# A two-layer decoder step on one core: each weight unit's matmuls in two groups, each behind its own wait

## The reference

```
h = rms_norm(x, norm_g)
z = h @ w_in                       # 2048 -> 14*512 + 8 + 4*2048 columns
y_ret, y_gdn, y_sc, y_pool = four token mixers on slices of z, each times its SiLU gate
proj  = einsum('btnc,ncd->btnd', ys, w_branch)       # four branches, 512 -> 2048
gates = sigmoid(merge_logits)                        # the last 4*2048 columns of z
out   = x + sum_n(gates * proj) @ w_out              # 2048 -> 2048
```

## Time and profile before

| | |
|---|---|
| time of three runs | 2048.74, 2050.52, 2054.93 us |
| the profiled execution | span 2049.6 us from first to last instruction; its own whole time is not listed, the median of the runs is 0.9 us above this span |
| PE | busy 1992.3 us, 97% of the span, 16294 matmuls and as many weight loads |
| DVE | busy 1346.1 us, 66% |
| ACT | busy 1113.6 us, 54% |
| transfers | 348 MB, 170 GB/s in the mean |
| granted TensorE clock | 0.993 of full in the mean |

### The profile page before, as it was taken

One profiled execution on the slowest core, in us unless ns is written; L12 is line 12 of the kernel. 1 busy time (PEld: TensorE's weight loads), 2 busy tenths in 40 slices (PEclk: granted clock), 3 DMA queues, 4 the chain that ended last, 5 costly groups with the idle time before them and its releaser, 6 DMA issues.

```text
span 2049.6 us, 50596 instructions
## 1 busy us (share of the span) xinstructions
PE 1992.3 (97%) x16294; PEld 1976.0 (96%) x16294; DVE 1346.1 (66%) x2608; ACT 1113.6 (54%) x2045; POOL 186.5 (9%) x345
## 2 busy tenths in 40 slices
PE   6999999999999999999999999999999999999996
PEld 6999999999999999999999999999999999999996
DVE  7887566755656556666678766676565656566666
ACT  5556556645455555555555655655464645455554
POOL 2111110110101010000011210001010100100000
PEclk9999999999999999999999999999999999999998
DMA  6655555555554545665656555655555555566664
GB/s 209 190 175 172 157 181 162 184 160 156 154 172 135 176 140 167 188 180 180 184 172 184 171 173 155 190 164 175 165 162 160 162 155 149 160 175 179 178 184 161
DMA packets 183252, 348.13 MB, mean 170 GB/s; under 512 B 20592, under 2 KB 20720, under 8 KB 182992
## 3 DMA queue, kind: packets, MB, share of 16 engines
q1 hardware_dynamic: 177552, 326.45, 53.4%
q0 software_dynamic: 5568, 19.80, 3.0%
HBM read 333.61 MB, written 12.56 MB: 169 GB/s over the span
## 4 chain that ended last, share of the span: by engine, by line
PE 90%; DVE 4%; issue 3%; ACT 2%; DMA 1%; DVEq 0%; ACTq 0%; SPq 0%
PE acc L1301 27%; PE acc L1302 27%; PE acc L1303 26%; DMA raw<-w_stream 1%; PE side L1514 1%; PE side L1488 1%; DVE wlo L829 1%; PE side L1512 1%; PE side L1505 1%; ACT whi L540 1%; PE side L1396 1%; PE side L1495 1%; PE side L1402 1%; PE side L1358 1%; DVE act_lo L841 0%
## 5 line engine op out<-in xcount | busy, mean ns | idle before, releaser
L829 DVE TENSOR_TENSOR wlo<-raw,whi 128x512 fp32r<-128x512 f32 x1219 | 828.3, 694 | 488.4 <-ACT whi L540 481.4
L540 ACT ACTIVATE whi<-raw 128x512 fp32r<-128x512 f32 x1219 | 751.5, 628 | 643.7 <-PE acc L1303 553.9
L1301 PE MATMUL acc<-act_hi,whi 128*128 128x264 f32 x3328 | 972.6, 292 | 40.1 <-issue 19.6
L1303 PE MATMUL acc<-act_hi,wlo 128*128 128x264 f32 x3328 | 947.8, 285 | 0.0
L1302 PE MATMUL acc<-act_lo,whi 128*128 128x264 f32 x3328 | 947.2, 285 | 0.0
L1301 PEld LDWEIGHTS acc<-act_hi,whi 128*128 128x128 f32 x3328 | 631.8, 190 | 48.2 <-issue 35.9
L1302 PEld LDWEIGHTS acc<-act_lo,whi 128*128 128x128 f32 x3328 | 632.8, 190 | 0.9
L1303 PEld LDWEIGHTS acc<-act_hi,wlo 128*128 128x128 f32 x3328 | 629.4, 189 | 0.0
L1301 PE MATMUL acc<-y_hi,whi 128*128 128x264 f32 x1536 | 439.9, 286 | 0.0
L1302 PE MATMUL acc<-y_lo,whi 128*128 128x264 f32 x1536 | 435.4, 283 | 0.0
L1303 PE MATMUL acc<-y_hi,wlo 128*128 128x264 f32 x1536 | 434.8, 283 | 0.0
(11 more groups left out here) (267 smaller groups left out, 1438.2 us busy)
## 6 DMA issues: line engine op xcount, KB each, us to landing
raw<-w_stream SPq DMA_DIRECT2D x1220, 256.0 KB, 2.8
state<-ret_in POOLq DMA_DIRECT2D x8, 512.0 KB, 5.5
s_ret<-state POOLq DMA_DIRECT2D x8, 512.0 KB, 4.6
state<-gdn_in POOLq DMA_DIRECT2D x8, 512.0 KB, 5.4
s_gdn<-state POOLq DMA_DIRECT2D x8, 512.0 KB, 6.1
x<-x_in SPq DMA_DIRECT2D x4, 528.0 KB, 6.5
y_out<-wide SPq DMA_DIRECT2D x4, 396.0 KB, 2.8
con<-consts SPq DMA_DIRECT2D x1, 1582.0 KB, 11.8
```

Of the source, the lines that this page charges most:

```text
L540: sc.activation(whi[:, s, :], raw[:, s, :], ACT.Copy).then_inc(hi_ready, 1)
L829: ve.tensor_tensor(wlo[:, s, :], raw[:, s, :], whi[:, s, :].bitcast(F32), ALU.subtract).then_inc(lo_ready, 1)
L1301: mm(acc[bank][:, 0:N], w_h, hi[:, k0 + k, :], start=first and k == 0, stop=False)
L1303: op = mm(acc[bank][:, 0:N], w_l, hi[:, k0 + k, :], start=False, stop=last and k == UK - 1)
```

## The change

Inside each unit the twelve matmuls are put in another order. The eight with the rounded weights come first, behind a wait for `hi_ready`; the four with the remainder come last, behind the wait for `lo_ready`. Nothing changes in ACT's, DVE's, POOL's and SyncE's programs, and the matmuls are the same ones.

```
-            def product(bank, slot, hi, lo, k0, first, last):
+            def product_hi(bank, slot, hi, lo, k0, first):

                 for k in range(UK):
-                    w_h, w_l = whi[:, slot, k * P:(k + 1) * P], wlo[:, slot, k * P:(k + 1) * P]
+                    w_h = whi[:, slot, k * P:(k + 1) * P]
                     mm(acc[bank][:, 0:N], w_h, hi[:, k0 + k, :], start=first and k == 0, stop=False)
                     mm(acc[bank][:, 0:N], w_h, lo[:, k0 + k, :], start=False, stop=False)
+
+            def product_lo(bank, slot, hi, k0, last):
+
+                for k in range(UK):
+                    w_l = wlo[:, slot, k * P:(k + 1) * P]
                     op = mm(acc[bank][:, 0:N], w_l, hi[:, k0 + k, :], start=False, stop=last and k == UK - 1)
                 op.then_inc(unit_used, 1)
...
                 def unit(j, bank, hi, lo, k0, first, last):
+                    pe.wait_ge(hi_ready, ub + j + 1)
+                    product_hi(bank, j % RING, hi, lo, k0, first)
                     pe.wait_ge(lo_ready, ub + j + 1 + RING)
-                    product(bank, j % RING, hi, lo, k0, first, last)
+                    product_lo(bank, j % RING, hi, k0, last)
                 return unit
```

## The result

The change makes the kernel slower: 2063.99 us in the median of 4 runs (2063.11 to 2065.85) against 2051.11 us of 4 runs of the kernel before (2048.74 to 2054.93). The ratio is 1.0063, with a 95% interval from 1.0048 to 1.0078. The forecast was 2042.6 us, and the range up to 2050.5 does not hold the result. The profiled execution has a span of 2064.2 us, 14.6 more than before; it is the longest of the four, and the medians lie 12.9 apart.

What follows compares the result with a forecast made beforehand. PE, busy 97% of the span, was taken as the bound. Gains of 9.0 us less 1.2 for the clock cut the span by 7.8, from 2049.6 to 2041.8; 0.9 above that gave about 2042.6 us, range 2037 to 2050.5.

Steps and rivals of the forecast that it cites:

- a change of weights and activations between two matmuls: Inside every unit: the reordering was claimed to cost no more than any step's 0.12 us, so 0 was added.
- The loops grow by four register rows and at least as many waits a pass: PE's loops: the added rows were feared only for making S's branch as slow as M's; taken as 0.
- the ends of M: Ends of the M passes: of eight stops of 0.20 us only two would be gained, 0.4 us.
- the clock: Behind the M branches: idles grow by 0.2 us, and half of one more half-clock spell was taken as a 1.2 us loss.
- the sum: All expected gains over the kernel: 5.8 + 0.8 + 0.7 + 0.4 + 1.3 = 9.0 us.
- The 13 named stops: PE's waits for wlo in stage P and at both layers' starts: all but two vanish, giving back 5.8 us.
- Unit 199: Second layer's counterpart included: whi itself is late, so the unit starts 0.26 us late and 0.37 us of its stop stays.
- The six stops in S: Fourth unit of each S pass, behind retention's matmuls: estimated 0.13 us each, 0.8 us gained.
- The fourth unit: First layer's start: eight matmuls run before wlo comes, the norm's matmul starts at 26.8; 1.3 us gained, between 0.9 and 1.8.
- The second wait: Between the eighth and ninth matmul of each of 1216 units: claimed to cost 0 when already met.
- the new wait costs in every unit: Rival, chance 0.06: the added wait keeps the ninth matmul's weights from loading ahead even when met; slower, up to 2164 us.

Runs made afterwards that it cites:

- e1: The changed order of matmuls, but with the one old wait for lo_ready at the unit's start: 2064.87 us, 1.0064 of the kernel before.
- e2: The kernel before's order of matmuls, with both waits (hi_ready at the unit's start, lo_ready ahead of its third matmul): 2061.42 us, 1.0046 of the kernel before.
- e5: No decoder step: TensorE alone runs several matmul orders and tile distances on constant data; 1.450 us a unit in the old order, 1.460 in the changed one.
- e3: The changed kernel with only loop M's first instruction put at slot 0 of a 256-instruction fetch block: 2055.69 us, 1.0025 of the kernel before.
- e4: The kernel before with only loop M's first instruction put at slot 222 of a 256-instruction fetch block: 2057.28 us, 1.0026 of the kernel before.
- e6: The kernel before with changed order and two waits only in units that used to stop, loop M's head at slot 0: 2049.69 us, 0.999 of before.
- e12: No decoder step: TensorE alone repeats 264-column matmuls with the same weights, only the activations' starts changing: 120.2 to 123.3 ns a step.
- the three groups: Order of four matmuls by hi, four by lo, four with the remainder; in the changed kernel with loop M's head at slot 0: 2043.99 us, 0.9953 of before.

## Why the prediction was wrong

**The failed steps are two costs taken as nothing.** One is "a change of weights and activations between two matmuls costs no more than the 0.12 of any step: 0". The row gave two decimals, and I used it for a sum over 14592 matmuls, in which 1 ns a step is 14.6 us. The step depends on what follows what: e1, e2 and e5 show 7.9 to 9.8 ns a unit more, which makes 10.7 us.

The other is "The loops grow by four register rows and at least as many waits a pass", with S's and M's branches as the only thing to fear: "I take 0, since S's pass stays far shorter than M's 60 units." I asked whether a short loop would become a long one. No loop did (S's branch takes 0.2 us still). What the rows did was to move the head of the loop that was long already; e3 and e4 show this both ways. The six edges cost 10.0 us more, 5.8 of them in second stops, where I had a gain of 0.4 at the ends of M and a loss of 1.2 for the clock.

10.7 + 10.0 - 14.6: the stops gave back 6.1 us in the profiled execution, against 8.6 in the sum (9.0 without the 0.4 at M's ends, which the edges hold). Term by term:

- *The 13 named stops.* Stage P and the layers' starts, 5.8 us. In P the mechanism and the size were right: no wait for `wlo` is left, and 1.57 + 0.31 for the 32 units' slower pace is 1.9 us a layer, where 2.0 follow from the sum. Unit 199 went as worked out:

```profile
349.97 0.19 PEld L1301 LDWEIGHTS acc<-act_hi,whi 128*128 128x128 f32 x1 [0.28 <-ACT whi L540]
349.97 0.39 PE L1301 MATMUL acc<-act_hi,whi 128*128 128x264 f32 x1
```

  It waits 0.28 us for `whi`, against 1.04 for `wlo`; 0.26 was forecast. At the second layer's start the stops are gone too, but units 608 and 609 run at the lower clock level for 1.5 us longer than before, and nothing is won.
- *The six stops in S*, 0.8 us: 0.6 a layer when the pace is taken out, and 0.44 a layer in e6, where the pace is the old one. Right.
- *The fourth unit.* PE does eight matmuls by 22.81 and waits for `wlo` as described; then:

```profile
26.16 1.25 PE L1308 MATMUL acc<-act_hi,wlo 128*128 128x264 f32 x4 [3.06 <-DVE wlo L829]
27.21 1.08 PE L1325 MATMUL side<-osq,con 128*128 128x264 f32 x2
```

  Four matmuls take 1.05 us, as worked out (1.04). The norm's matmul starts at 27.21 and not at 26.8 because DVE ran 0.4 us later in this execution; before it was 28.56. Unit 4 then ran 0.8 us longer, at the lower clock level, so that unit 5 began 0.5 us earlier than before, or 0.9 without DVE's delay, against 1.3 in the sum. The mechanism was right, and the size at its lower end.
- *The second wait*, 0 when met: right inside a unit (e2).
- *The clock.* I took 2.94 to 3.05 us of idle time as the border. There is no such border. Stretches behind four edges of the changed kernel (us, busy PE, granted clock, DMA share, GB/s):

```profile
607.30:608.90 1.60, 1.56 (x13) 1.00 0.36 134
717.20:718.80 1.60, 1.58 (x13) 1.00 0.73 245
1510.50:1512.50 2.00, 2.00 (x10) 0.55 0.55 179
1620.50:1622.50 2.00, 2.00 (x9) 0.50 0.16 55
```

  Ahead of them PE was idle for 3.05, 3.70, 2.59 and 3.78 us. The first two are followed by the upper level (2.4 GHz), the shortest and the longest by the lower (1.2 GHz) in most of the stretch or all of it. What decides it is not shown. The clock took some 1.3 us at the edges and 1.5 at the second layer's start, against the 1.2 in the sum.

Of the rivals, "the new wait costs in every unit" had the right side, and 7.9 to 9.8 ns a unit lie inside its prices (from 7 ns a unit it eats the gain, from 12 ns the kernel is slower by over 0.3%). That is luck: the wait is free and the order is not, and at this price a unit the kernel would be about as fast as before. The 0.6% came from the edges as well. It got a chance of 0.06, since I weighed only whether the wait hides, and no rival held that the same matmuls in another order could run at another pace.

## What to carry to other kernels

Where a change touches every step of the engine that sets the time, take the step from a stretch of many units to a tenth of a nanosecond, not from neighbouring rows: here 1 ns a step is 0.7% of the kernel. Try the orders on that engine alone first; one profile of them (e5) would have picked the three groups.

Adding a few instructions ahead of a long loop can cost as much as what they are for, through the place of the loop's head alone (8.3 us between the changed kernel and e3). Hold that place fixed when two versions are compared, and look at the stop behind each long back branch before anything smaller: here six of them were worth 25 us or more, against the 8 to 11 that the split gives at its best.

## What the runs showed of the hardware that was not expected

- The pace of 264-column matmuls at the upper clock level depends on where their activations start and on the order of the starts: in e5 120.0 ns a step with tiles 1536 bytes apart, 120.8 and 121.7 for the old and the new order with tiles 1056 bytes apart; 120.2 to 123.3 in e12. In e5 the units' times repeat within 3 ns every four units, and no other engine is needed.
- A long loop's back branch can need two fetches in sequence. At the edge shown PE restarts 4.2 and 7.6 us after the branch begins in e4, 4.8 and 8.2 in the changed kernel, so the second is hidden only if the head lies far enough ahead of the block's end: 30 and 34 instructions were too few at five and three of six edges, 69 were enough.
- With the back branch announced, M's branches take 0.2 us, and 54 fewer packets of code are fetched, nine for each of the six edges: a loop of 1811 instructions (before) is then not fetched again for its later passes.
